# Moving 32 of 64 columns in the block-wise triangular inverse of a gated delta stage

## The reference, cut to what matters

```python
C = 64                                     # chunk; 8 heads, head size 128; 256 prompt + 64 sample tokens
kb = k * beta[..., None]
lower = where(strict, einsum('bhncd,bhnsd->bhncs', kb, k) * exp(diff), 0.0)
m = lower + eye(C)
u = triangular_solve(m, v * beta[..., None], left_side=True, lower=True, unit_diagonal=True)
w = triangular_solve(m, kb * exp(gc)[..., None], left_side=True, lower=True, unit_diagonal=True)
```

## Time and profile before

| | |
|---|---|
| median of 3 runs | 1734.4 us (1733.68 to 1738.12) |
| the profiled execution | 1737.15 us |
| its span | 1735.4 us |
| TensorE busy in the span | 1595.9 us (92%) |
| VectorE, ScalarE, GpSimd busy | 1159.9, 961.2, 93.6 us |
| mean granted TensorE clock | 0.959 of full |
| level loop (L1286, L1300, L1303) | about 232 to 312 us |

### The profile page before, as it was taken

How to read it: one execution, slowest core, us unless ns; L and a number is a source line. 1 busy time by engine, 2 the same in 40 slices (tenths; PEclk the granted TensorE clock), 3 DMA queues, 4 the chain that set the end, 5 groups by cost and what they waited for, 6 DMA issues and landing times. The chain is left out here.

```text
span 1735.4 us, 25615 instructions
## 1 busy us (share of the span) xinstructions
PE 1595.9 (92%) x10479; PEld 1341.5 (77%) x10479; DVE 1159.9 (67%) x1224; ACT 961.2 (55%) x1167; POOL 93.6 (5%) x193
## 2 busy tenths in 40 slices
PE   6999899957999997997779999999999999999993
PEld 3999466647999997994576888888888888888882
DVE  3775621168444456445676888888888888888884
ACT  2553421266333435333566777777777777777772
POOL 2210100000000000000002010010101010000001
PEclk8999899978999998998889999999999999999997
DMA  9720989473554354339035999999999999999983
GB/s 322 227 73 27 352 307 357 161 220 93 152 155 147 126 154 146 98 98 384 17 103 214 364 361 385 370 378 370 373 379 364 382 360 386 360 375 355 381 317 105
DMA packets 267290, 446.87 MB, mean 257 GB/s; under 512 B 12614, under 2 KB 125455, under 8 KB 267151
## 3 DMA queue, kind: packets, MB, share of 16 engines
q1 hardware_dynamic: 262812, 430.53, 71.2%
q0 software_dynamic: 3632, 13.11, 2.1%
q10 hardware_dynamic: 720, 1.50, 0.3%
HBM read 420.64 MB, written 24.47 MB: 256 GB/s over the span
## 5 line engine op out<-in xcount | busy, mean ns | idle before, releaser
L2687 DVE TENSOR_TENSOR w_lo_late<-raw,w_hi_late 128x2048 fp32r<-128x2048 f32 x262 | 598.0, 2290 | 102.5 <-ACT w_hi_late L2581 100.9
L2581 ACT ACTIVATE w_hi_late<-raw 128x2048 fp32r<-128x2048 f32 x262 | 502.1, 1917 | 157.7 <-PE bank L356 157.7
L354 PE MATMUL bank<-w_hi_late,hg_hi 128*128 128x512 f32 (+1 forms) x768 | 291.8, 380 | 0.0
L356 PE MATMUL bank<-w_hi_late,hg_lo 128*128 128x512 f32 (+1 forms) x768 | 289.7, 377 | 0.0
L355 PE MATMUL bank<-w_lo_late,hg_hi 128*128 128x512 f32 (+1 forms) x768 | 288.0, 375 | 0.0
L275 DVE TENSOR_TENSOR w_lo_main<-raw,w_hi_main 128x2048 fp32r<-128x2048 f32 (+1 forms) x50 | 112.4, 2250 | 88.5 <-ACT w_hi_main L268 88.5
L356 PEld LDWEIGHTS bank<-w_hi_late,hg_lo 128*128 128x128 f32 x768 | 144.5, 188 | 29.2
L355 PEld LDWEIGHTS bank<-w_lo_late,hg_hi 128*128 128x128 f32 x768 | 144.3, 188 | 28.8
L354 PEld LDWEIGHTS bank<-w_hi_late,hg_hi 128*128 128x128 f32 x768 | 144.2, 188 | 27.7 <-issue 0.5
L354 PE MATMUL bank<-w_hi_late,act_hi 128*128 128x512 f32 x352 | 141.1, 401 | 0.0
L356 PE MATMUL bank<-w_hi_late,act_lo 128*128 128x512 f32 x352 | 139.9, 398 | 0.0
(11 more groups left out here) (509 smaller groups left out, 2796.4 us busy)
## 6 DMA issues: line engine op xcount, KB each, us to landing
raw<-in_moe_w_gate SPq DMA_DIRECT2D x88, 1024.0 KB, 7.4
raw<-in_moe_w_up SPq DMA_DIRECT2D x88, 1024.0 KB, 7.5
raw<-in_moe_w_down SPq DMA_DIRECT2D x88, 1024.0 KB, 6.9
ada_delta<-in_ada_w SPq DMA_DIRECT2D x40, 1024.0 KB, 8.9
raw<-in_gdn_w_in SPq DMA_DIRECT2D x16, 1024.0 KB, 10.3
slot_rows_far<-zero_row SPq DMA_DIRECT2D x1, 12288.0 KB, 39.3
raw<-in_ffn_w_gate SPq DMA_DIRECT2D x22, 512.0 KB, 4.1
raw<-in_ffn_w_up SPq DMA_DIRECT2D x22, 512.0 KB, 5.3
```

Source lines behind the costliest of these rows:

```text
L354: pe.matmul(out, w_hi, x_hi, start=start, stop=False)
L356: return pe.matmul(out, w_lo, x_hi, start=False, stop=stop)
L2581: act.activation(k.w_hi[:, m % SPL, :], k.raw[:, m % RAW, :], ACT.Copy).then_inc(k.hi_ready, 1)
L2687: dve.tensor_tensor(k.w_lo[:, m % SPL, :], k.raw[:, m % RAW, :], k.w_hi[:, m % SPL, :], ALU.subtract).then_inc(k.raw_split, 1)
```

## The change

At level n the columns of the 64 that change lie in runs: of every 2s columns, the first s of `w` (and so of X') hold the new block, and the second s of `w` are identity columns; in the transpose Y' it is the second s that change. Two helpers, `first_of` and `second_of`, pick these columns as a four-dimensional view. With them

- `product` moves only the first columns of `x` (32 per head, in 16 runs of 2 at level 1, one run of 32 at level 5), and VectorE masks only these;
- the second columns of `w`, which equal the mask, are copied by GpSimd from `masks`, one copy per step, with a semaphore `w_filled` for which `update` waits; GpSimd waits, as VectorE does, for the update of step j - 3;
- `update` computes only the first columns of X' and the second columns of Y', and ScalarE copies only these;
- in the last level of units 0 and 1 the half of `y` that does not change is copied into `inv` by two extra instructions ahead of the wait for the update.

The weight tiles keep their 64x64 shape, and the number of matmuls is the same. The modulation units are untouched.

```diff
         l_off = [words(8192 + 512 * c, 512)[0:HALF].rearrange("p (h n) -> p h n", n=HALF) for c in range(2)]
         et, ug, eg = (words(9216 + 1024 * n, 1024) for n in range(3))
         last_state = [words(1024 * n, 1024).rearrange("p (h n) -> p h n", n=DK) for n in range(2)]
-        diff_done = sem("diff_done")
+        diff_done, w_filled = sem("diff_done"), sem("w_filled")
         gc_sum, nb_ready, gcol_exp, ug_ready, rows_done = (sem(n) for n in (
             "gc_sum", "nb_ready", "gcol_exp", "ug_ready", "rows_done"))
         et_exp, et_ready, eg_ready, tail_sum, tail_ready, gram_done = (sem(n) for n in (
@@ -1186,6 +1186,12 @@
         def part_of(h):
             return both[h // 4], h % 4
 
+        def first_of(a, n):
+            return a.rearrange("p h (c two s) -> p h c two s", two=2, s=2 ** n)[:, :, :, 0, :]
+
+        def second_of(a, n):
+            return a.rearrange("p h (c two s) -> p h c two s", two=2, s=2 ** n)[:, :, :, 1, :]
+
         def item(n, u):
             return 3 * (n - 1) + u
 
@@ -1280,27 +1286,29 @@
                     pe.wait_ge(v_ready, 3)
                 if j >= 2:
                     pe.wait_ge(w_ready, j - 1)
-                bank = by64(p_bank(j))
+                bank, moved = first_of(by64(p_bank(j)), n), first_of(x[u], n)
                 for h in range(heads_of[u]):
                     for rs in both:
-                        last = pe.matmul(bank[rs, h, :], lt[u][rs, h, :], x[u][rs, h, :], start=True, stop=True)
+                        last = pe.matmul(bank[rs, h], lt[u][rs, h, :], moved[rs, h], start=True, stop=True)
                 last.then_inc(p_done, 1)
 
             def update(j):
                 n, u = steps[j]
                 pe.wait_ge(w_ready, j + 1)
+                pe.wait_ge(w_filled, j + 1)
                 if j >= 2:
                     pe.wait_ge(xy_ready, j - 1)
                 else:
                     pe.wait_ge(k_ready, 3)
                     pe.wait_ge(at_done, 3)
                 bx, by = (by64(t) for t in xy_banks(j))
+                bx, by, w_first, y_second = first_of(bx, n), second_of(by, n), first_of(w[u], n), second_of(y[u], n)
                 for h in range(heads_of[u]):
                     for rs in both:
-                        pe.matmul(bx[rs, h, :], y[u][rs, h, :], w[u][rs, h, :], start=True, stop=True)
+                        pe.matmul(bx[rs, h], y[u][rs, h, :], w_first[rs, h], start=True, stop=True)
                 for h in range(heads_of[u]):
                     for rs in both:
-                        last = pe.matmul(by[rs, h, :], w[u][rs, h, :], y[u][rs, h, :], start=True, stop=True)
+                        last = pe.matmul(by[rs, h], w[u][rs, h, :], y_second[rs, h], start=True, stop=True)
                 last.then_inc(xy_done, 1)
 
             def off(c):
@@ -1517,7 +1525,9 @@
                 if j >= 3:
                     dve.wait_ge(xy_done, j - 2)
                 nh = heads_of[u]
-                dve.tensor_tensor(w[u], by64(p_bank(j), nh), k.masks[:, n, :].unsqueeze(1).to_broadcast([P, nh, HALF]), ALU.mult).then_inc(w_ready, 1)
+                got, into = first_of(by64(p_bank(j), nh), n), first_of(w[u], n)
+                mask = first_of(k.masks[:, n:n + 1, :], n)
+                dve.tensor_tensor(into, got, mask.to_broadcast([P, nh, HALF // 2 ** (n + 1), 2 ** n]), ALU.mult).then_inc(w_ready, 1)
                 k.ada_dve(dve, 1)
                 k.ada_dve(dve, 1)
                 if j == 0:
@@ -1558,6 +1568,12 @@
                     if n == 0:
                         k.pool_chain.on(pool)(last)
                 last.then_inc(diag_ready, 1)
+            for j, (n, u) in enumerate(steps):
+                if j >= 3:
+                    pool.wait_ge(xy_done, j - 2)
+                nh = heads_of[u]
+                pool.tensor_copy(second_of(w[u], n), second_of(k.masks[:, n:n + 1, :], n).to_broadcast([P, nh, HALF // 2 ** (n + 1), 2 ** n])).then_inc(
+                    w_filled, 1)
 
         @block.scalar
         def _(act):
@@ -1613,15 +1629,19 @@
             first(2)
             k.ada_act(act, 8)
             for j, (n, u) in enumerate(steps):
-                act.wait_ge(xy_done, j + 1)
                 nh = heads_of[u]
                 bx, by = (by64(t, nh) for t in xy_banks(j))
-                act.activation(x[u], bx, ACT.Copy)
                 if n == LEVELS and u < S:
-                    for rs in both:
-                        last = act.activation(inv[u][rs, :, rs], by[rs, :, :], ACT.Copy)
+                    act.wait_ge(xy_ready, j - 2)
+                    for part, rs in enumerate(both):
+                        act.activation(inv[u][rs, :, HALF * part:HALF * part + HALF // 2], y[u][rs, :, 0:HALF // 2], ACT.Copy)
+                act.wait_ge(xy_done, j + 1)
+                act.activation(first_of(x[u], n), first_of(bx, n), ACT.Copy)
+                if n == LEVELS and u < S:
+                    for part, rs in enumerate(both):
+                        last = act.activation(inv[u][rs, :, HALF * part + HALF // 2:HALF * part + HALF], by[rs, :, HALF // 2:HALF], ACT.Copy)
                 else:
-                    last = act.activation(y[u], by, ACT.Copy)
+                    last = act.activation(second_of(y[u], n), second_of(by, n), ACT.Copy)
                 last.then_inc(xy_ready, 1)
                 k.ada_act(act, 1)
                 k.ada_act(act, 1)
```

## The result

The changed kernel takes 1765.5 us (median of 4 runs, 1760.7 to 1781.1) against 1735.7 us for the kernel before in the same series (1733.7 to 1738.1). The ratio is 1.0189, with a 95% interval of 1.0161 to 1.0218: slower by some 30 us. The forecast was 1732.8, range 1725 to 1740, with 0.10 for slower. The profiled execution is the slowest of the four, 1781.11 us with a span of 1779.4, 44.0 above the span before. The mean clock of the whole span is 0.929; the three other runs have 0.938 to 0.943, so the loss differs from run to run. Two executions in the series of the experiments, of 2321 and 4014 us, were slow ones and are left out of medians and ratios.

A forecast was written before the change was run, and what follows sets the result against it. TensorE was taken to set the pace of the delta stage's level loop, transfers just behind. Shorter idle times (1.4 us) and earlier-ending last matmuls (0.2) took 1.6 us off 1734.4, giving 1732.8 us, range 1725 to 1740.

The forecast's parts named there:

- The halved matmuls: Product and updates in the level loop: 32 moving columns keep the 28 ns load pitch of 64-wide weights, gain zero.
- The masks, the copies: VectorE's full masks fall from 0.688 to 0.419 us, a pair of ScalarE copies from 0.97 to 0.56.
- the gap: TensorE's idle time of 1.68 us where a modulation group ends, twice in the loop: 0.41 us shorter each.
- the hidden fills: GpSimd's fifteen new copies of identity columns: 0.33 to 1.4 us for a full one, hidden within about 9 us.
- the early copies: ScalarE's four extra copies of the unchanged half into the inverse: 0.38 us each, hidden ahead of its wait.
- The sum of 1.6 us: Total saving in the level loop: 1.4 us from shorter idle times plus 0.2 from earlier-ending last matmuls.
- I take the two as cancelling: TensorE's clock in the loop: shorter gaps (fewer falls) and thinner matmuls (more falls) offset each other, net zero.
- third rival: Clock falls more in the loop: one further fall a level at 1.7 us, 8.5 us added, 1741.3 us; chance 0.07.
- The row that I leaned on: Profile at 344 to 346 us: 64 columns move behind 128-wide loads, half the array's capacity, and the clock stays 1.00.
- The first rival: Moving side sets the pitch of the loop's matmuls: up to 17 us less, 1715.8 to 1724 us; chance 0.11.
- the floor of about 25 ns: Trainium skill's least start-to-start distance of matmuls; by it the 28 ns could fall by 3, some 4 us.
- The second: Rival: shorter gaps no longer bring clock falls in the loop, 1.6 and up to 5.6 us less, 1727.2; chance 0.08.

The follow-up runs named there:

- narrow-weights kernel: Changed kernel with only the first 32 of each 64 weight columns, mask a maximum and copies scaled by 1/64: 1732.8 us, ratio 0.9993.
- a_full_moving: Changed kernel with product and updates again moving all 64 columns, the rest of the change kept: 1733.55 us, ratio 0.9999.
- i_no_gap_half: Changed kernel with ScalarE's modulation row copy one unit earlier and VectorE's bias one unit later, 32 moving columns kept: 1743.3 us, ratio 1.0039.
- c_scattered_64: Kernel before, still moving all 64 columns but in scattered order, in product and both updates: 1733.4 us, ratio 1.0005.
- b: Changed kernel with the 32 columns taken as one run at every level, which computes another product: 1766.9 us, ratio 1.0179.
- d: Changed kernel with the identity columns written by VectorE ahead of its mask instead of by GpSimd: 1771.3 us, ratio 1.0207.
- e: Changed kernel with the product alone moving all 64 columns, the updates 32: 1737.7 us, ratio 1.0023.
- f: Changed kernel with both updates moving all 64 columns, the product 32: 1734.3 us, ratio 0.9999.
- g: Changed kernel with matmuls moving 64 columns at levels 1 to 3 and 32 at levels 4 and 5: 1750.2 us, ratio 1.0085.
- h: Changed kernel with matmuls moving 32 columns at levels 1 and 2 and 64 from level 3 on: 1748.8 us, ratio 1.0075.
- j: Changed kernel with all 64 columns moved, ScalarE's modulation work one unit earlier and VectorE's one unit later: 1727.1 us, ratio 0.9961.
- l: Kernel before with only ScalarE's modulation work one unit earlier and VectorE's one unit later: 1725.7 us, ratio 0.9952.

## Why the prediction was wrong

**Right.** The halved matmuls gain nothing: "Cutting the moving side to 32 leaves the load of 64 columns, and with it 28 ns" holds in the profile after, and the narrow-weights kernel shows why. The masks, the copies, the gap (0.43 us shorter against 0.41) and the hidden fills came out as costed; the early copies, 0.42 us each instead of 0.38, are hidden too. The sum of 1.6 us was tested by a_full_moving, which has all of it but the halved matmuls: its timeline shows the shorter gaps, its time is level with before, within an interval too wide for so little.

**Wrong: the clock.** The step that failed is "I take the two as cancelling", in the part on the clock. Shorter gaps against thinner matmuls were set equal on one row for thin work and none that weighs the one against the other. The prediction named the direction as its third rival, with a chance of 0.07, and priced it at one further fall a level of 1.7 us each, 8.5 us; it took the price of a fall from the kernel before, where dense matmuls bring the clock back soon. What was mis-sized is the length of a fall: in the changed kernel the first one lasts 119 us. A fall has a beginning and an end, and I asked only what begins it. In the profiled run it cost 43.3 us, in the four runs 25 to 45, against the forecast of none.

**The row that I leaned on** for thin work, at 344 to 346 us, moves 64 columns behind 128-wide loads at a clock of 1.00. It shows that a clock that is up can stay up for some microseconds of thin work. That is true in the loop after as well (1.00 from 230 to 236, and 34 us in i_no_gap_half). It doesn't show that a clock that is down comes back under such work, and the stretch is some 3.5 us long where the loop is 80.

**The cause, as far as the runs go.** Shown: the number of moving columns per matmul at an unchanged pitch is what brings the long half clock (a and c against b and d); it acts by degree, but not in proportion (e, f); the fall comes with the thin matmuls and ends with them within a run (g, h); no idle gap is needed right ahead of it, and with the gaps at the turns taken away the loss is a fraction, 7 to 9 us of some 30 (i). The Trainium skill, page "TensorE: Matmul & The Clock Gate", section "HAM oscillation — how this bites in real kernels", lays such falls to waits in which TensorE is idle. The trace agrees with it in part for the kernel before: its falls vanish with the gaps at the turns, though idle times of 1.32, 1.38 and 1.68 us passed without one. It disagrees for the thin matmuls: i_no_gap_half has 50 us at half clock with TensorE busy for 50.00 of them. But a profile shows 32 matmuls as busy for 1.10 us whether they move 64 columns or 32, so its busy time can't tell a full array from a thin one. Not settled: why i_no_gap_half's clock rises at 286 and not elsewhere, and why the runs of one kernel differ by 20 us; no row here shows what the chip goes by.

**The first rival,** faster by 17 us with the moving side as the limit, is refuted: no group became shorter. Nor did the floor of about 25 ns hold that it cites: with 32-wide weights in two quarters the distance is 15 ns. Its chance of 0.11 was what the missing row (64-wide weights, fewer than 64 moving) was worth. The second, a clock that stops falling, came true only with the gaps at the turns gone, in j and l; with gaps of 1.25 us the falls stayed (0.91 in two stretches of a_full_moving).

## What to carry to other kernels

Fewer moving columns shorten a matmul only down to the width of its weights; below that they leave the time and thin the array's work, and a clock that has fallen may not return until dense work does. Before cutting work on an engine that is bound by something else, ask what the cut does to the clock of that engine, and price a fall by how long the new work would hold it, not by how long the old did. Where TensorE idles for a microsecond at a hand-over, look for an instruction of another engine that can be put ahead of a wait: here one unit's shift on ScalarE and VectorE gave 0.5% with no work removed.

## What the runs showed of the hardware

- Load-to-load distance is 15 ns for 32-wide weights, 28 for 64-wide, in two quarters of the array in turn, both with 32 moving columns.
- The granted clock stood at 0.50 for 119 us while TensorE was busy for 116.8 of them; with matmuls of 64 columns moved at the same pitch it stood at 0.93 (0.94 with the product alone halved).
- Under thin work the clock held either level: 50 us at half, then 34 us at full, with the same instructions and no idle time in the first stretch.
- With 32 moving columns the clock fell for 119 us behind 64-wide weights (a load every 28 ns), and stayed at 1.00 for 15 us behind the same gap with 32-wide ones (every 15 ns).
- Gaps of 1.25 to 1.68 us at the turns were mostly followed by falls under matmuls of 64 columns, and without these gaps the loop ran at 1.00. But gaps of 1.68 us (c_scattered_64), 1.38 and 1.32 us (with the shift) passed with the clock at 1.00.
